# Mixer inverses: ten level products in 32x32 diagonal tiles instead of 64x64

## The reference

```python
S = (S * w_t[:, :, None, :]
     - jnp.einsum('bhvk,bhk->bhv', S, kk_t)[..., None] * (kk_t * a_t)[:, :, None, :]
     + v_t[..., None] * k_t[:, :, None, :])
o_t = jnp.einsum('bhvk,bhk->bhv', S, r_t)
```

## Time and profile before

| | us |
|---|---|
| median of three runs | 3073.42 |
| the three runs | 3067.15, 3073.42, 3073.47 |
| the profiled execution, its own time | 3073.63 |
| its span, first to last instruction | 3071.8 |
| TensorE busy | 2916.8 (95% of the span) |
| VectorE, ScalarE, GpSimd busy | 2081.7, 1253.7, 331.0 |
| the eight passes of the mixer | 397 (749 to 1146) |

### The profile page before, as it was taken

How to read it: one execution, slowest core, us unless ns; L and a number is a source line. 1 busy time by engine, 2 the same in 40 slices (tenths; PEclk the granted TensorE clock), 3 DMA queues, 4 the chain that set the end, 5 groups by cost and what they waited for, 6 DMA issues and landing times.

```text
span 3071.8 us, 56681 instructions
## 1 busy us (share of the span) xinstructions
PE 2916.8 (95%) x24302; PEld 2407.3 (78%) x24302; DVE 2081.7 (68%) x2378; ACT 1253.7 (41%) x1569; POOL 331.0 (11%) x550
## 2 busy tenths in 40 slices
PE   5899999977999979999999999999889999999999
PEld 2488888735888868888888888899667888888887
DVE  3587776566778756787877878679865555555554
ACT  2322221156565634444434443366344434334342
POOL 1000000002344310112121221000000000000000
PEclk9799999988999989999999999999989999999999
DMA  9986887694000037688888888455245666565653
GB/s 319 350 294 219 304 315 276 232 376 156 25 16 25 16 72 237 224 286 303 286 286 292 287 287 299 171 181 188 74 137 156 201 194 190 192 188 187 191 186 126
DMA packets 306041, 640.77 MB, mean 209 GB/s; under 512 B 19035, under 2 KB 23937, under 8 KB 303585
## 3 DMA queue, kind: packets, MB, share of 16 engines
q1 hardware_dynamic: 269280, 529.94, 51.4%
q0 software_dynamic: 28384, 94.76, 9.2%
q10 hardware_dynamic: 8128, 12.46, 1.1%
HBM read 623.55 MB, written 13.40 MB: 207 GB/s over the span
## 4 chain that ended last, share of the span: by engine, by line
PE 75%; DMA 9%; DVE 9%; issue 5%; ACT 2%; POOL 0%; ACTq 0%; SPq 0%; DVEq 0%; POOLq 0%
PE ps L470 41%; PE ps L509 12%; PE ps L511 6%; DMA line<-in_ada_w_dram 3%; DMA raw<-in_ada_w_dram 3%; PE ps L1791 3%; DVE line L2139 2%; PE ps L489 2%; DMA late<-in_ada_w_dram 2%; DVE split_lo L447 1%; PE ps L2664 1%; PE ps L407 1%; PE ps L1913 1%; PE ps L1694 1%; PE ps L3216 1%
## 5 line engine op out<-in xcount | busy, mean ns | idle before, releaser
L447 DVE TENSOR_TENSOR split_lo<-raw,split_hi 128x2048 fp32r<-128x2048 f32 (+1 forms) x372 | 849.3, 2285 | 465.7 <-ACT split_hi L435 458.2
L435 ACT ACTIVATE split_hi<-raw 128x2048 fp32r<-128x2048 f32 x368 | 701.0, 1911 | 1077.5 <-PE ps L470 761.3
L509 PE MATMUL ps<-xa,split_hi 128*128 128x512 f32 x2048 | 722.6, 398 | 4.2 <-ACT xa L668 4.2
L511 PE MATMUL ps<-xa,split_lo 128*128 128x256 f32 x2048 | 573.1, 280 | 0.0
L509 PEld LDWEIGHTS ps<-xa,split_hi 128*128 128x128 f32 x2048 | 385.9, 188 | 98.9 <-ACT xa L668 4.5
L511 PEld LDWEIGHTS ps<-xa,split_lo 128*128 128x128 f32 x2048 | 387.3, 189 | 0.2
L470 PE MATMUL ps<-split_hi,hT_hi 128*128 128x512 f32 x992 | 387.1, 390 | 0.0
L470 PE MATMUL ps<-split_hi,hT_lo 128*128 128x512 f32 x992 | 386.0, 389 | 0.0
L470 PE MATMUL ps<-split_lo,hT_hi 128*128 128x512 f32 x992 | 386.0, 389 | 0.0
L470 PEld LDWEIGHTS ps<-split_hi,hT_hi 128*128 128x128 f32 x992 | 186.2, 188 | 40.2 <-issue 1.8
L470 PEld LDWEIGHTS ps<-split_hi,hT_lo 128*128 128x128 f32 x992 | 186.2, 188 | 38.9
(11 more groups left out here) (439 smaller groups left out, 4466.3 us busy)
## 6 DMA issues: line engine op xcount, KB each, us to landing
raw<-in_mlp_w_dram SPq DMA_DIRECT2D x256, 1024.0 KB, 5.6
raw<-in_ada_w_dram SPq DMA_DIRECT2D x64, 1024.0 KB, 8.8
raw<-in_mix_in_w_dram SPq DMA_DIRECT2D x48, 1024.0 KB, 5.8
raw<-in_conv_pw_w_dram SPq DMA_DIRECT2D x48, 1024.0 KB, 5.6
gate<-in_ada_w_dram SPq DMA_DIRECT2D x172, 256.0 KB, 5.0
line<-in_ada_w_dram POOLq DMA_DIRECT2D x171, 256.0 KB, 4.8
late<-in_ada_w_dram POOLq DMA_DIRECT2D x85, 256.0 KB, 4.9
tmpa<-in_ada_w_dram SPq DMA_DIRECT2D x84, 256.0 KB, 4.9
```

Of the source, the lines that this page charges most:

```text
L435: nc.scalar.activation(split_hi[:, c, :, 0:n], raw[:, c, :, 0:n], ACT.Copy).then_inc(hi_done, 1)
L447: nc.vector.tensor_tensor(split_lo[:, c, :, 0:n], raw[:, c, :, 0:n], split_hi[:, c, :, 0:n], ALU.subtract).then_inc(lo_done, 1)
L509: pe.matmul(ps[:, base + j, :], split_hi[:, c, kk, j * P:(j + 1) * P], both, start=(k == 0), stop=False, skip_group_check=True)
L511: mm = pe.matmul(ps[:, base + j, 0:SEQ], split_lo[:, c, kk, j * P:(j + 1) * P], xa_hi[:, k, :], start=False, stop=(k == KT - 1), skip_grou ...
```

## The change

The ten updates with `k < NT_DVE` (= 10, block sizes n = 1, 2, 4, 8, 16) leave out the two 32x32 squares of `rw_mt` off the diagonal, which are zero. Each 64x64 by 64-column matmul becomes two matmuls with 32x32 weights. The moving matrix is triangular too: one of the two needs 64 - n columns ("wide"), the other 32 - n ("narrow"). Groups of four wide and four narrow matmuls alternate; the four of a group lie in the four diagonal 32x32 tiles of the array, and all write to the same bank. An update has 32 matmuls instead of 16. Updates 10 and 11 stay as they were. Nothing else changes: same waits, same signals, same order.

```diff
+        rows32 = lambda e, c: slice(e * HB + c * HB // 2, e * HB + (c + 1) * HB // 2)
...
-                for i in range(8):
-                    for e in range(2):
-                        z = strict_scores(b)[own_half(e), i // 4, i % 4, :] if k < 2 else R["zz"][own_half(e), b, i, :]
-                        mm = pe.matmul(ps[own_half(e), ZB[b], i * HB:(i + 1) * HB], R["mt"][own_half(e), b, i, :], z,
-                                       start=False, stop=True, skip_group_check=True)
+                if k >= NT_DVE:
+                    for i in range(8):
+                        for e in range(2):
+                            mm = pe.matmul(ps[own_half(e), ZB[b], i * HB:(i + 1) * HB], R["mt"][own_half(e), b, i, :], R["zz"][own_half(e), b, i, :],
+                                           start=False, stop=True, skip_group_check=True)
+                    mm.then_inc(W["z_lev"], 1)
+                    return
+                n = 1 << (k // 2)
+                for i in range(0, 8, 2):
+                    for wide in (1, 0):
+                        for o in range(2):
+                            for e in range(2):
+                                d = (e + o) % 2
+                                c = d if wide else 1 - d
+                                q = rows32(e, c)
+                                t = slice(0, (c + 1) * HB // 2 - n) if d else slice(c * HB // 2 + n, HB)
+                                z = strict_scores(b)[q, (i + o) // 4, (i + o) % 4, t] if k < 2 else R["zz"][q, b, i + o, t]
+                                mm = pe.matmul(ps[q, ZB[b], (i + o) * HB + t.start:(i + o) * HB + t.stop], R["mt"][q, b, i + o, rows32(0, c)], z,
+                                               start=False, stop=True, skip_group_check=True)
                 mm.then_inc(W["z_lev"], 1)
```

## The result

The changed kernel takes 3084.69 us in the median of 11 runs (3076.42 to 3089.89), the kernel before 3072.09 (3066.04 to 3077.07): ratio 1.0036 with the interval 1.0023 to 1.0049, some 11 us slower. That is inside the range of 3058 to 3090, but 9 us above the predicted 3076, and at 0.36% it is outside the 0.2% that was the likeliest case. The profiled execution took 3084.69 us with a span of 3082.9, against 3073.63 and 3071.8.

The account below looks back on a forecast made before the run. TensorE's updates 1 to 9 were taken to bound each mixer pass; the array's 21.6 us saving was lost to instruction fetch, level stretch 18.5 us, 0.3 more, eight passes +2.4 on 3073.63: 3076, range 3058 to 3090.

Parts of the forecast that it names:

- the likeliest case: Mixer: the instruction fetch eats the array's gain, total within about 5 us of +2.4; chance 0.42.
- What the array would save: Updates 1 to 9 of each mixer pass: 2.7 us saved a pass, 21.6 us in eight passes.
- L2664: Mixer updates: 32x32 records come no faster than that line's 19.5 ns, update 1.25 us, total 3096; chance 0.08.
- the bank: Mixer updates: four tiles on one bank take turns, 1.6 us more an update, +118, total 3192; chance 0.02.
- 8 x (0.83 x (96 - 2n) + 10): Array time of a changed update, 0.71 to 0.51 us for n = 1 to 16, against 0.93.
- Instructions in blocks: Mixer levels: TensorE's program comes in 256-instruction blocks, T = 3.8 us each when waited for; 20 blocks more.
- the fetch doesn't bind: Mixer levels: fetches stay ahead, all 21.6 us gained, 3052; chance 0.1, within 0.27 for both faster forms.
- Eight passes: +2.4: Mixer: level stretch 18.5 us, 0.3 more than now, in each of eight passes; 3076 in all.
- The granted clock: Mixer: waits of one to two microseconds could also bring the clock down; no size given.
- Block limits behind the mixer fall where they fell: Behind the mixer: the ten updates add 5120 instructions, exactly 20 blocks, so limits there don't move.
- The 12.5 us in 17 times: All mixer passes: TensorE's idle time before L1791, waiting for the transpose, mostly at update 1.
- the fetch binds harder: Mixer: T as in the convolution, 4.1 us a block, +10 us, 3084; chance 0.21.

Follow-up runs that it names:

- 64x32 kernel: Kernel before with each of the ten updates split into 32 matmuls of 64x32 weights, all 64 columns moving: 3087.75 us, ratio 1.0026 to before.
- cut columns: Kernel before, 64x64 weights and 16 matmuls an update, but only the 64 - n nonzero columns moving: 3073.42 us, ratio 1.0004 to before.
- wide only: Changed kernel without its narrow matmuls, so part of the inverse is left out: 3048.01 us, ratio 0.9897 to before.
- spread: Kernel before with 32x32 tiles in updates 1, 2, 3, 5, 8, 9, all passes but the last: 3063.03 us, ratio 0.9945; again 3057.92, 0.9946.
- only the last pass: 32x32 form in the last pass alone, passes 0 to 6 as in the kernel before: 3072.37 us, ratio 1.0004 to before.
- half a block more: Kernel before with the 32x32 form in updates 8 and 9 of the first pass, 128 instructions more: 3066.26 us, ratio 0.9967 to before.
- the quarter block: Spread kernel with update 7 of the first pass also in 32x32 form, 64 instructions more: 3067.71 us, ratio 0.9973 to the kernel before.
- half-less kernel: Changed kernel with the old form in updates 0 and 4 of the first pass, 128 instructions fewer: 3084.78 us, ratio 1.0027 to the kernel before.

## Why the prediction was near, and where it failed

**What the array would save: right, a little large.** From the starts of the records, unbroken updates of 64 take 0.70, 0.70, 0.68, 0.66 and 0.62 us to their last start for n = 1, 2, 4, 8, 16, about 0.01 more with the last; forecast were 0.71, 0.69, 0.67, 0.61, 0.51. So 11 ns a record, and none of the rivals L2664 (19.5) or the bank. The term that is off is "8 x (0.83 x (96 - 2n) + 10)". With wide records alone an update takes 0.43 us for n = 1 and 0.34 for n = 16, in proportion to the columns; the narrow ones add 0.27 and 0.28, about 34 ns each whether they have 31 columns or 16. Nine updates save 2.25 us a pass, 18 in all, not 21.6.

**Instructions in blocks: right.** 20 packets more, waits that cut the program every 127 or 128 matmul records, limits 3.9 us apart (T = 3.8), 22.6 us more of waiting on issue in the mixer where the sum implied 21.6 + 2.4 = 24.0. Passes 3 to 7 are 0.35 us longer in the mean, forecast 0.3. The two crossed experiments show the mechanism: the instructions without the tiles cost 8 us, the tiles without the instructions (and without the narrow records) give 32. The rival in which the fetch doesn't bind is out. The Trainium skill's page "Runtime: NRT & Kernel Launch", section "Instruction fetch mechanics", by which the crossing of a block is mostly hidden, holds where a block lasts 6 us, as in the levels of the kernel before, which show no such wait, and not for the levels after.

**"Eight passes: +2.4": this step failed.** It took a pass without other DMA traffic for all eight; the mixer as a whole became 20.0 us longer. In the last pass the fetch starts late beside the broadcasts, and one block took 6.7 us: that pass alone is 8.0 us longer, and its waits on issue from 1101 to 1129 sum to 8.9 us (10.1 in the whole pass) where before had one of 1.1. The wait of 3.4 us for GpSimd that before had there is gone, and the array saves its 2.2; the 12 us more at the lower clock are worth up to 6. In the 64x32 kernel, without these 12, the waits alone made it as long. Four kernels that double instructions there agree (59.0 to 61.1 us), and all those that leave that pass in its old form or with no more instructions have 51.1 to 53.2. I had read the DMA share of the mixer as a mean (0.12 in the earlier trace rows) and not by pass.

**The granted clock: named as a danger, given no price.** The mixer has 47 us at the lower level in the profile after, 19 in that of before: 29 more at half speed, worth up to 14 us. With it the account roughly closes: 23.8 us more of waits on issue in the eight passes, less 3.8 of other waits, less 18 from the array, plus up to 14, is up to 16. Before each wait the last record, about 0.2 us, also runs out alone where it would else overlap the next; for 25 waits on issue more (31 against 6) that is an estimated 5 us. The mixer is 20.0 longer. TensorE is busy for 361 us of the eight passes before and 360 after, and idle 20 and 40: what the array saves is taken back by those ends and by slower records at the lower clock.

What brings the clock down is not settled. The rows show what TensorE did before it fell. In the profile after, the granted clock falls at 787.3, 1101.3, 1118.4 and 1125.2, next to the ends of four waits on issue of 1.6 to 2.7 us (785.9, 1101.4, 1118.1 and 1124.8), and a last time at 1149.1, behind one of 1.2 us that ends at 1146.7. Over all fourteen profiles, 36 of the 37 falls within the eight passes come during a wait of TensorE of 0.9 us or more or within 2.5 us of its end; the exception is one in the 64x32 kernel. (The two limits are those of this count, and none of the chip's.) But most such waits, 76 of 112, are followed by no fall: the wait at 932.6 to 933.7 in the kernel before is not, the same wait in cut columns is. So more waits may well be why after has 47 us. Against it stands that the time varies without the change: cut columns has no instruction more and 34 us, wide only few waits on issue and 40, spread 37 in one profile and 17 in the next of the very same kernel. That these 29 us belong to the change is not shown.

**"Block limits behind the mixer fall where they fell": right, and worth more than I thought.** The ten updates add exactly 20 blocks, and the taps of after (53.8 us) stay in the group of before (52.6 to 55.4). What was not foreseen is that any kernel which moves them by half a block is 2 to 6 us faster there (5 against the unchanged kernel). It accounts for two misses: only the last pass, +7 - 5 = +2 against a measured +1; and the spread form, where six updates in seven passes save 7 x 1.5 = 10.5 us by the array and 5 us in the taps, 16 against 17. For half a block more it gives 0.6 + 5.5 = 6 against 10 measured (interval 5.5 to 15), for the quarter block, against the spread form, 4 us slower against 8. Those two are larger in the medians than in the taps; what else moves with the limits stays open.

**A reading of the earlier trace rows that was too large.** The 12.5 us in 17 times that TensorE is said to wait for the transpose are the waits before matmuls (4.5 us, 8 times) and those before weight loads (8.0 us, 9 times) added, though they lie in the same time. That only strengthens the point made with it.

**Where luck helped.** The likeliest case, that the fetch eats the gain, was the mechanism. The size was four to five times the forecast (11 us against 2.4), and in the mixer, the only place that the sum is about, eight times (20.0). The total stayed in the range partly because what lies before and behind the mixer was 9 us shorter in this profile, for reasons that the prediction didn't have and the record only explains in part. The rival "the fetch binds harder" named 3084, the time measured, but by a T of 4.1 us in all eight passes; passes 2 to 7 had a level stretch of 18.6 us in the mean, near the 18.5 of the main case and not 19.5. Its number came out by another way: the late fetches of one pass, and the clock, of which that rival had said that it could fall.

## What to carry to other kernels

A denser form of the same work pays only as long as a block of 256 instructions (64 float32 matmuls, with two matmul records and two loads each) still lasts longer than its fetch, about 3.9 us here and up to 6.7 beside heavy DMA traffic: count instructions per microsecond before and after, stretch by stretch, and look at the DMA share of each stretch, not at its mean. Put the dense form where its neighbours are sparse: six of ten updates, spread out, gave 0.55% where all ten lost 0.36% (the spread kernel also left the last pass alone and had the better block position, which is worth about 5 of its 17 us). And when a kernel has any stretch that waits for instructions, a change far ahead of it moves the block limits in it; add or take half a block before a difference of 0.2 or 0.3% is put down to the change itself.

## What was unexpected of the hardware

- The position of the block limits: 49.8 to 50.6 us against 52.6 to 55.4 for the same 1736 matmuls of the taps, in 13 of 13 profiles by half a block's shift.
- Four row and column tiles of 32x32 write to one bank at 11 ns a record, so they don't take turns; the page "TensorEngine Tiling (Array Packing)" of the Trainium skill, section "Restrictions and Gotchas", says that different row tiles can't, and the measurement decides for this layout, in which each tile writes its own partitions.
- An instruction fetch beside 1 MB broadcasts held TensorE up for 2.4 to 2.7 us a time in the profile after, and up to 4.5 us in that of the half-less kernel, against 0.4 to 1.6 us elsewhere in the mixer. The fetch itself was no slower; it started 3.9 to 4.4 us after the block before it was begun, instead of 1.1 to 1.8.
- Of 37 falls of the granted clock in the passes, 36 came with or soon behind a wait of TensorE of 0.9 us or more, but only 36 of 112 such waits were followed by one.
- Leaving out a quarter of the moving columns of a 64x64 tile (48 instead of 64) changed its update from 1.15 to 1.14 us.
